# A change in the first stage of a two-layer kernel: the order of its loads and of the operands made from them

## The reference

```python
c_act = jax.nn.silu(c)                                  # (1, 2048)
mod = c_act @ w_ada[l] + b_ada[l]                       # 2048 x 12288
sh_a, sc_a, gt_a, sh_f, sc_f, gt_f = [m[:, None, :] for m in jnp.split(mod, 6, axis=-1)]
h = _rmsnorm(x, norm_mix[l]) * (1.0 + sc_a) + sh_a      # 256 x 2048
p = h @ w_in[l]                                         # 2048 columns in, 9296 out
c_q, c_kv, k_pe, q_g, k_g, v_g, z, b_logit, a_logit, gate_logits = _split_cols(p)
```

## Time and profile before

| | |
|---|---|
| median of three executions | 2225.25 us |
| profiled execution, its own time | 2224.08 us |
| its span, first to last instruction | 2222.5 us |
| TensorE matmul busy | 2180.3 us, 98% |
| TensorE weight load busy | 1830.0 us, 82% |
| VectorE busy | 1504.1 us, 68% |
| ScalarE busy | 1004.1 us, 45% |
| mean granted TensorE clock | 0.996 |
| moved from and to memory | 507.08 MB, mean 228 GB/s |

### The profile page before, as it was taken

The page is one execution under the profiler, slowest core; times in us unless marked ns, Lnnn a source line. Parts: engine busy times, 40 slices in busy tenths (PEclk is TensorE's granted clock), DMA queues, the critical chain, the costliest instruction groups (busy, mean ns, idle before and its releaser), DMA issues.

```text
span 2222.5 us, 27221 instructions
## 1 busy us (share of the span) xinstructions
PE 2180.3 (98%) x10552; PEld 1830.0 (82%) x10552; DVE 1504.1 (68%) x1891; ACT 1004.1 (45%) x1284; POOL 24.1 (1%) x26
## 2 busy tenths in 40 slices
PE   6899999999999999999999999999999999999998
PEld 5798988888888888888888888878888888888887
DVE  8989698988788667756455555575556555655556
ACT  5356445434444644443444434464444444444444
POOL 0001000000000000000000000000000000000000
PEclk9999999999999999999999999999999999999999
DMA  9975577876998678865665666565666666566663
GB/s 404 420 275 156 181 233 254 292 257 238 332 345 298 222 262 293 291 225 189 197 190 186 188 199 190 186 217 177 193 192 192 185 195 193 186 191 191 194 188 129
DMA packets 241553, 507.08 MB, mean 228 GB/s; under 512 B 19305, under 2 KB 34961, under 8 KB 235921
## 3 DMA queue, kind: packets, MB, share of 16 engines
q1 hardware_dynamic: 241424, 505.35, 68.7%
HBM read 503.16 MB, written 2.12 MB: 227 GB/s over the span
## 4 chain that ended last, share of the span: by engine, by line
PE 81%; DVE 9%; DMA 5%; issue 2%; ACT 2%; POOL 0%; DVEq 0%; SPq 0%; ACTq 0%; POOLq 0%
PE bank L1240 25%; PE bank L1242 25%; PE bank L1241 25%; DVE WL L2064 3%; PE bank L1172 1%; DVE RAW L2051 1%; PE bank L1431 1%; DMA RAW<-in_w_ada_dram 1%; DVE A L2241 1%; ACT WH L1514 1%; DMA RAW<-in_w_cd_dram 1%; DMA A<-in_w_cd_dram 1%; PE bank L1247 1%; DMA RAW<-in_w_cq_dram 1%; PE bank L1249 1%
## 5 line engine op out<-in xcount | busy, mean ns | idle before, releaser
L2064 DVE TENSOR_TENSOR WL<-RAW,WH 128x1024 fp32r<-128x1024 f32 x706 | 860.3, 1223 | 579.5 <-ACT WH L1514 570.5
L1514 ACT CAST WH<-RAW 128x1024 fp32r<-128x1024 f32 x706 | 738.6, 1050 | 851.8 <-PE bank L1242 713.5
L1240 PE MATMUL bank<-WH,HTh 128*128 128x512 f32 x1922 | 757.4, 394 | 1.0 <-DVE WL L2064 1.0
L1242 PE MATMUL bank<-WH,HTl 128*128 128x512 f32 x1922 | 748.9, 390 | 0.0
L1241 PE MATMUL bank<-WL,HTh 128*128 128x512 f32 x1922 | 748.2, 389 | 0.0
L1240 PEld LDWEIGHTS bank<-WH,HTh 128*128 128x128 f32 x1922 | 361.0, 188 | 76.0 <-DVE WL L2064 2.4
L1242 PEld LDWEIGHTS bank<-WH,HTl 128*128 128x128 f32 x1922 | 360.8, 188 | 76.2
L1241 PEld LDWEIGHTS bank<-WL,HTh 128*128 128x128 f32 x1922 | 361.2, 188 | 72.5
L1240 PE MATMUL bank<-WH,R2h 128*128 128x512 f32 x408 | 160.4, 393 | 0.7 <-DVE WL L2064 0.7
L1242 PE MATMUL bank<-WH,R2l 128*128 128x512 f32 x408 | 159.0, 390 | 0.0
L1241 PE MATMUL bank<-WL,R2h 128*128 128x512 f32 x408 | 158.9, 389 | 0.0
(11 more groups left out here) (301 smaller groups left out, 1821.0 us busy)
## 6 DMA issues: line engine op xcount, KB each, us to landing
RAW<-in_a_w_in_dram SPq DMA_DIRECT2D x192, 512.0 KB, 3.8
RAW<-in_w_gate_up_dram SPq DMA_DIRECT2D x176, 512.0 KB, 4.5
RAW<-in_w_ada_dram SPq DMA_DIRECT2D x128, 512.0 KB, 5.6
RAW<-in_w_in_dram SPq DMA_DIRECT2D x112, 512.0 KB, 5.2
RAW<-in_w_down_dram SPq DMA_DIRECT2D x88, 512.0 KB, 4.3
RAW<-in_a_w_out_dram SPq DMA_DIRECT2D x64, 512.0 KB, 3.9
A<-in_w_ada_dram SPq DMA_DIRECT2D x17, 1024.0 KB, 14.0
RAW<-in_w_o_dram SPq DMA_DIRECT2D x32, 512.0 KB, 6.1
```

Source lines behind the costliest of these rows:

```text
L1240: e.matmul(o, ah[:, s], hi[:, k, :], start=first, stop=False)
L1242: i = e.matmul(o, al[:, s], hi[:, k, :], start=False, stop=last)
L1514: e.copy(hi, rv).then_inc(S["hi"], 1)
L2064: e.tensor_tensor(lo, rv, hi.bitcast(F32), ALU.subtract).then_inc(S["lo"], 1)
```

## The change

It does the following, all in the first stage:

- The units of a group come block by block: scale row and shift row of its first block, then of its second (`plan_units`). The ckv and conv weights of the group before stay behind the group's first row.
- In the last group the weights of block 15 come last, behind its rows, and its shift row is loaded as two halves of 512 KB, reduced one after the other. There is one unit more, so the last user of slot 0 is now the cq load of block 15, that of slot 1 its `w_cd` load.
- `cam` is made for one block as soon as its two rows are reduced. ScalarE's part of `h` becomes a step of its own for one block (`hk`), right behind that `cam`: the float32 operand first, then the high half. The cq split of the group stands behind `hk` of its last block. VectorE's part of `h` stays where it was.
- `cs` on TensorE waits for one block's operand at a time.
- In the last group the splits of block 15 stand behind `h`.

```diff
         for gi, (k0, n) in enumerate(GROUPS):
-            g = [("g", 16 + k0 + k) for k in range(n)] + [("g", k0 + k) for k in range(n)]
+            g = [("g", c + k0 + k) for k in range(n) for c in (16, 0)]
+            if gi + 1 == NG:
+                g[-1:] = [("g", k0, 0), ("g", k0, 1)]
             u.append(g[0])
             if last:
                 u.append(("w", ckv) + last)
             last = (k0, n)
+            u.extend(g[1:] + [("w", cq) + last])
             if gi + 1 == NG:
-                u.extend([("w", cq) + last, ("w", ckv) + last] + g[1:])
-            else:
-                u.extend(g[1:] + [("w", cq) + last])
+                u.append(("w", ckv) + last)
...
             if gi == 2:
                 self.put("rope_tables")
+            self.front_ada()
             if gi + 1 == NG:
-                self.front_split(cq)
-                self.front_split(ckv)
-                self.front_split(conv)
-            while self.ga_n < 2 * (k0 + n):
                 self.front_ada()
-            self.put("cam", gi)
+            self.put("cam", k0)
+            self.put("hk", gi, k0)
+            if n == 2:
+                self.front_ada()
+                self.front_ada()
+                self.put("cam", k0 + 1)
+                self.put("hk", gi, k0 + 1)
             if gi + 1 < NG:
                 self.front_split(cq)
         self.put("h", NG - 1)
+        self.front_split(cq)
+        self.front_split(ckv)
+        self.front_split(conv)
...
-            W.wait_ge("xmod", k0 + n)
             for k in range(n):
+                W.wait_ge("xmod", k0 + k + 1)
...
-        elif kind == "h":
-            gi, = args
-            k0, n = GROUPS[gi]
-            W.wait_ge("cam", gi + 1)
-            W.wait_ge("xt_e", (k0 + n + 1) // 2)
-            for kt in range(k0, k0 + n):
-                e.activation(L.HTh[:, kt, :], L.XT0[:, kt, :], ACT.Identity, scale=L.cAm[:, kt:kt + 1],
-                             bias=L.cBm[:, kt:kt + 1]).then_inc(S["ht_hi"], 1)
+        elif kind == "hk":
+            gi, kt = args
+            at = kt - GROUPS[gi][0]
+            W.wait_ge("cam", kt + 1)
+            W.wait_ge("xt_e", kt // 2 + 1)
             W.wait_ge("ht_lo", gi - 1)
             W.wait_ge("cs", gi - 1)
-            for kt in range(k0, k0 + n):
-                e.activation(L.tmp1[gi % 2][:, (kt - k0) * T:(kt - k0 + 1) * T], L.XT0[:, kt, :], ACT.Identity,
-                             scale=L.cAm[:, kt:kt + 1], bias=L.cBm[:, kt:kt + 1]).then_inc(S["xmod"], 1)
+            e.activation(L.tmp1[gi % 2][:, at * T:at * T + T], L.XT0[:, kt, :], ACT.Identity,
+                         scale=L.cAm[:, kt:kt + 1], bias=L.cBm[:, kt:kt + 1]).then_inc(S["xmod"], 1)
+            e.activation(L.HTh[:, kt, :], L.XT0[:, kt, :], ACT.Identity, scale=L.cAm[:, kt:kt + 1],
+                         bias=L.cBm[:, kt:kt + 1]).then_inc(S["ht_hi"], 1)
...
         elif kind == "cam":
-            gi, = args
-            k0, n = GROUPS[gi]
-            s = slice(k0, k0 + n)
-            W.wait_ge("ga_dve", 2 * (k0 + n))
-            e.scalar_tensor_tensor(out=L.cAm[:, s], in0=L.MOD[:, 16 + k0:16 + k0 + n], scalar=1.0, in1=L.colNM[:, s],
+            kt, = args
+            s = slice(kt, kt + 1)
+            W.wait_ge("ga_dve", sch.ga_of[kt])
+            e.scalar_tensor_tensor(out=L.cAm[:, s], in0=L.MOD[:, 16 + kt:17 + kt], scalar=1.0, in1=L.colNM[:, s],
                                    op0=ALU.add, op1=ALU.mult).then_inc(S["cam"], 1)
```

More of the change, by code:

```diff
@@ L509, in front_ada @@
     def front_ada(self):
-        self.ada(self.staged[0], self.units[self.staged[0]][1])
+        self.ada(self.staged[0], *self.units[self.staged[0]][1:])
         self.issue_loads()
@@ L1086 @@
 CELL = count_cells()
-RAW1_FREE = (("lo", 3 * NG), ("ga_dve", 32))
+RAW1_FREE = (("lo", 3 * NG), ("ga_dve", 33))
 def half_need(sch, j, kt, tt):
```

## The result

The changed kernel takes 2235.43 us (median of six, 2235.15 to 2236.74), the kernel before 2225.59 us beside it: ratio 1.0048, 95% interval 1.0038 to 1.0058 (the two medians by themselves give 1.0044). It is 9.8 us slower, under half a percent.

A forecast was written before the change was run, and what follows sets the result against it. It took transfers to bound the first stage before, VectorE with ScalarE in its chain after; 11.3 us over the groups plus 0.5 us at the stage's end made 11.8 us, hence 2237 us as a median, range 2231 to 2240 us.

The forecast's parts named there:

- The stretch: Page slices: DMA full only in the first two, TensorE nearly full in all the others.
- What bounds the stage: First stage: VectorE, with ScalarE in its chain, replaces the bytes (14.83 us a group) as the bound.
- The wait in front of the cq low half: VectorE in each group waits for two activations and the cq cast: 2.22 us in place of 0.50.
- The sum for a group: VectorE per group: 13.64 own work + 0.36 cam + 2.22 wait = 16.22 us, 1.39 us longer.
- How it adds up: Lag by group: +2.0 us first, +2.37 second, 5 x 1.39 third to seventh; 11.3 us at the eighth.
- The end of the stage: From group eight's first reduction to the next job: 25.25 us against 24.78, waiting for w_ct; 0.5 us later still.
- Behind the stage: After the next job's first matmul: no further lag was added to the 11.8 us.
- rival C: More than the sum: low TensorE clock or late weights behind w_ct add 3 us, 2240 us; chance 13 percent.
- The total: Whole kernel: 11.3 + 0.5 = 11.8 us slower, 2237 us as a median.
- Rival A: First stage: transfers stay the bound, VectorE's wait fits its margin; 1.1 us gained, 2224 us; chance 10 percent.
- Rival B: After the stage: TensorE's idle time up to 400 us absorbs up to 4.9 us, 2232 us; chance 15 percent.
- The DMA share: DMA from 40 to 110 us: share falls to near 0.93 from 1.02.

The follow-up runs named there:

- e2: Kernel before with only ScalarE's four activations of h moved right behind cam, ahead of the group's cq split: 2239.07 us, ratio 1.0064.
- e1: Changed kernel with the cq split moved ahead of the last block's hk on ScalarE in each group: 2226.43 us, ratio 1.0006.
- e3: Changed kernel with one activation instead of two ahead of the cq cast, the high-half one moved behind it: 2232.03 us, ratio 1.0033.
- e8: Changed kernel with the next job's first two loads (w_ct) put into the halves of slot 2 instead of slot 0: 2232.16 us, ratio 1.0034.
- e4: Changed kernel with the last group as in the kernel before, block 15's weights ahead of its whole shift row: 2233.14 us, ratio 1.0040.
- e7: Changed kernel with the cq split ahead of the last block's hk and w_ct loaded into slot 2: 2223.89 us, ratio 0.9997.
- e9: Changed kernel with cq split ahead of hk, VectorE's low part of h early, w_ct in slot 2, block 15's shift row whole: 2222.16 us, ratio 0.9988.

## Why the prediction was right, and where its sizes were off

- *The stretch.* The text ahead of the prediction, and the prediction with it, have the DMA engines full only in the first two of the forty slices. The page shows nine tenths in the eleventh and twelfth too (332 and 345 GB/s, against 404 and 420), with TensorE at nine tenths or more there. For the first stage nothing changes by it.
- *What bounds the stage.* Right: with 1.2 us of margin in a group, VectorE became the bound. e2 shows the cause by itself, e1 shows it by taking it away, e3 by its dose.
- *The wait in front of the cq low half.* Forecast 2.22 us, measured 2.17 to 2.20 in the second to seventh group, with the two activations and the cast in it as named.
- *The sum for a group.* Forecast 16.22 us, measured 15.77. The mis-sized terms: cam costs 0.20 us (98.56 to 98.76, last instruction of the reduction to the start of the next) and not the 0.36 that I took, so the low bound was the value; VectorE's own work was overstated by 0.16 us, since the reduction behind the cq low half starts 1.15 us after it (105.77 to 106.92) and not 1.31 as in the earlier trace rows, and by 0.09 us in the low part of h (0.60, not 0.69). I had read 0.08 us behind the subtraction as a property of the order; it is there where the transfers set the pace (e1: 112.47 + 1.23 to 113.77) and gone where VectorE does (e2: 109.49 + 1.23 to 110.63). Why isn't shown.
- *How it adds up.* Forecast 11.3 us at the eighth group, measured 8.82: 1.98 in the first group (forecast 2.0), 2.13 in the second (2.37), and 0.94 on average in the other five (1.39).
- *The end of the stage.* The count from that reduction to the next job was 25.25 us, measured 25.03 (122.69 to 147.72), and the w_ct gate was the last to open, as forecast.
- *Behind the stage.* This the forecast had wrong: it took the lag at the next job's first matmul for the lag at the end and put what follows at nothing, and 3 us more came. They stood in rival C, priced at 3 us for two mechanisms together. The low clock had no part in it that shows: the granted clock was 1.00 from 120 us on (above). The other, weights behind the first w_ct load that come late, is what happened, and cost 3.1 us where I gave it 1.3: not TensorE's own waits (0.76 and 0.30 us) but VectorE's queue behind the second w_ct load carries it. The counts from group eight to the conv chain in e8 and e4 show it.
- *The total.* The traces' 12.5 us are 8.8 + 0.25 + 3 and small changes later; my 11.8 us had 2.5 too much in the groups and about as much too little behind them. That these cancel is luck. The medians' 9.8 us are less than both, because the two profiled executions lay on opposite sides of their medians; in which stretch those 2.8 us lie isn't shown.
- *Rival A.* It did not happen in the change. e7, which meets its condition (a wait of 0.31 us), shows its size: no gain that can be told from none, though its interval doesn't exclude the 1.1 us priced; the conv chain in its trace is not earlier than before. The rule of the Trainium skill named there ("Perfetto Trace Analysis", Optimizing Scalar/DVE Operations) shows no gain here by breaking up h alone (e7, ratio 0.9997); a gain came only with the early low part of h, the open gate and the whole shift row as well (e9).
- *Rival B.* Nothing was given back: the lag was 9.07 us at the next job's first matmul (138.65 us before), 12.1 us where TensorE waits for VectorE (169.60 before), and 12.5 us at the end.
- *The DMA share.* I said that it would fall to 0.93 from 40 to 110 us; it stayed 1.02. That was wrong: in the stretch up to 115 us the lag was taken out of the transfers under way. Of the rows issued between 85 and 112 us before, and 85 and 120 us after, the median time to landing fell from about 14 to under 8 us:

```profile
A<-in_w_ada_dram SPq DMA_DIRECT2D x4, 1024.0 KB, 14.1
```
```profile
A<-in_w_ada_dram SPq DMA_DIRECT2D x5, 1024.0 KB, 7.9
```

## What to carry to other kernels

When a step that waits is moved ahead of one that doesn't on an in-order engine, add up what then stands between the awaited event and the other engine's next need; here two activations and a cast, 2.2 us, came to stand between VectorE's cam and its own next instruction. A stage whose transfers are at share 1.02 may still have a second engine with only 1.2 us of margin in 14.8, and what a repeated wait adds beyond that margin is paid in each group. A slot's last user is a gate: putting the last weights behind the rows also moved the next job's first loads behind them, and in the traces that cost a third as much again (3.1 us on 9.07).

## What was not expected of the hardware

A full DMA share didn't say here that transfers were the bound. In the changed kernel it stood at 1.02 and 420 GB/s from 40 to 115 us, while from 26 to 115 us neither VectorE nor the ScalarE instructions that it waits for were held by a transfer; the time from issue to landing, 7.9 us in place of 14.1, told the difference. The granted clock fell after TensorE's wait of 3.71 us before 110.02 us: it was 0.50 from 111.2 to 114.2 us, the lower level of 1.2 GHz. No cost of it shows, since TensorE stood again for VectorE afterwards (2.12 us before 125.79).
